# Group norm after retention: centring the value rows instead of the prompt's outputs

## Chip, core and metric

The kernel is one launch on one core of a Trainium2 chip. The metric is the device time of the launch in microseconds; lower is better. Three executions of the kernel before gave 679.87, 680.28 and 681.02 us, a median of 680.28 us.

## What is computed

A step of a two-layer hybrid network over 256 prompt tokens and 8 sample tokens, all in float32. Each layer has an input projection, three branches (a diagonal state-space model, called S5, stick-breaking attention, and retention), an output projection, a layer norm and a gated convolutional feed-forward with another layer norm. The change is in retention and the group norm behind it:

```python
def retention_chunk(s, q, k, v):
    ...
    inner = jnp.einsum('blhd,bmhd->bhlm', q, k) * decay
    o = jnp.einsum('bhlm,bmhe->blhe', inner, v)
    ...
def retention_branch(q, k, v, g, pos, s0, gn_g, gn_b):
    ...
    mu = jnp.mean(o, -1, keepdims=True)
    var = jnp.mean(jnp.square(o - mu), -1, keepdims=True)
    o = ((o - mu) * lax.rsqrt(var + LN_EPS)).reshape(bn, L, RET_WIDTH) * gn_g + gn_b
    return jax.nn.silu(g) * o, s_new
```

There are 4 heads with 128 values each (`e` above). For the prompt the starting state is zero, so an output row is a weighted sum of value rows. For the samples the old state, of 64 x 128 per head, is added.

## The kernel before, in words

Activations lie transposed: 128 features on the partitions, T = 264 tokens on the free axis (columns 0 to 255 the prompt, 256 to 263 the samples). A weight unit is a 128 x 1024 piece of weights. Units come by DMA into a ring of five buffers (`ring`). ScalarE casts a unit to `w_hi` (`split_hi`) and VectorE subtracts to get `w_lo` (`split_lo`), and each product is then three matmuls, on lines 429 to 431. The 20 units of the input projection are the exception: most go straight from the ring (line 422), four in layer 1 are split early (`EARLY`, lines 441 to 443).

Everything is written out by hand, engine by engine: each engine has its own program, in its own order, and semaphores tie them. `need(engine, name, L, k)` waits until `name` has been counted k times in layer L. `claim(bank, reader, ...)` makes TensorE wait until the last reader of a PSUM bank is done. The table `AT` says after which unit of the input projection each piece of the branches is put. No planner moves anything.

Names that the steps below use:

- `transposes` (TensorE, lines 568 to 575) turns the prompt's values into token rows in banks 4 and 5; `v_tokens` (ScalarE, line 1134) copies them to `VT`.
- `s5_glu` puts two products in banks 2 and 3, and ScalarE reads both with a sigmoid (line 1236). `k_transposes` (line 593) claims bank 2 afterwards, `v_samples` (line 584) follows it on TensorE.
- `ret_out` (lines 656, 657) multiplies the decayed scores `RI` with `VT`; ScalarE copies the outputs to `Oh` (line 1264). `ret_samples_turn` (line 648) turns the samples' part in bank 6, and `sample_out` (VectorE, lines 1762, 1766) adds it into `Oh` and frees the bank (`osamp`).
- `gn_means` (line 665) multiplies `Oh` with a matrix of 1/128 in four banks. `gn_center` (line 1863) subtracts the result, ScalarE squares (line 1278) and `gn_vars` (line 671) averages the squares.
- `square_sum` (line 1868) and `rms` (line 566) do the norms of the other two branches in the same stretch.
- `conv_prev` (lines 1804 to 1807) prepares the samples' old convolution rows, `spre`, which the feed-forward stage reads some 40 us later.
- The branches' results are split into `cat_hi` (ScalarE, line 1155) and `cat_lo` (VectorE, line 1881), eight pieces each. The output projection (lines 429 to 431) takes its first three units over pieces 0 to 3, then over 4 to 7, and waits for each piece of `cat_lo`.

Of the kernel before, what the change touches and what calls it, by code (L numbers as in the profile page):

```python
# [24 lines left out]
ALU = mybir.AluOpType  # L25
ACT = mybir.ActivationFunctionType

P = 128
SEQ, NS = 256, 8
T = SEQ + NS  # L30
# [76 lines left out]
def hybrid_step(nc, A, O):  # L107
    with ExitStack() as ctx:
# [53 lines left out]
        we_hi = [at(f"we_hi{e}", [P, 8, P], over=(home, plane * HJ * T), dt=F32R)  # L162
                 for e, (home, plane) in enumerate((("work", 0), ("work", 1), ("turn", 0), ("turn", 1)))]
        tabs = [(turn[:, 0, :, 0:SEQ], turn[:, 1, :, 0:SEQ]), None]
        RI = at("RI", [P, HEADS, DEC])
        KD = at("KD", [P, 2, 256])
# [46 lines left out]
        steps = at("steps", [P, SEQ])  # L213
        kdec = at("kdec", [P, 2, HEADS])
        gam = at("gam", [P, 1])
        gcol = at("gcol", [P, RAW, 2])
# [49 lines left out]
        def need(eng, name, L, k):  # L266

            eng.wait_ge(S(name), L * PERL[name] + k)

        def in_bank(i):  # L270
# [7 lines left out]
                "vb": 2, "vbev": 2, "rin": 4, "ri": 4, "rstate": 1, "rso": 1, "srg": 1, "sr": 1, "qs": 5,  # L278
                "rsq": 1, "otev": 1, "rot": 1, "osamp": 1, "ro": 4, "oev": 4, "gmean": 4, "gd": 4, "gsq": 4,
                "gvar": 4, "gv1": 1, "gr": 1, "gsil": 2,  # L280
# [119 lines left out]
        def _(pe):  # L400
# [250 lines left out]
            def ret_out(L):  # L651
                need(pe, "vt", L, 2)
                for h in range(HEADS):
                    need(pe, "ri", L, h + 1)
                    bank = claim(OUT_BANK[h], "oev", L, h + 1)
                    mm(bank[:, 0:SEQ], VT[:, 0, h * DV:(h + 1) * DV], RI[:, h, 0:SEQ], start=True, stop=False)
                    E.did(mm(bank[:, P:SEQ], VT[:, 1, h * DV:(h + 1) * DV], RI[:, h, SEQ:DEC], start=False, stop=True),
                          "ro")

            def gn_means(L):  # L660
                need(pe, "osamp", L, 1)
                for h in range(HEADS):
                    need(pe, "oev", L, h + 1)
                    bank = claim(4 + h, "gd", L, h + 1)
                    E.did(mm(bank[:, 0:T], C["mean_v"], Oh[:, h], start=True, stop=True), "gmean")  # L665

            def gn_vars(L):
                for h in range(HEADS):
                    need(pe, "gsq", L, h + 1)
                    bank = claim(4 + h, "gv1", L, 1)  # L670
                    E.did(mm(bank[:, 0:T], C["mean_v"], sqo[:, h], start=True, stop=True), "gvar")  # L671
# [94 lines left out]

            pe.wait_ge(S("warm"), 1)
            warm(WARM[0])
# [4 lines left out]
            for L in range(DEPTH):  # L773
# [7 lines left out]
                for i in range(RAW, N_IN):  # L781
# [41 lines left out]
                    if L == 0 and i == at_["out"]:  # L823
                        ret_out(L)
                    if i == at_["rt"]:
                        ret_samples_turn(L)
                    if i == at_["yt"]:
                        sb_values_turn(L)
                    if L > 0 and i == at_["vt"]:
                        transposes(L)  # L830
                    if L > 0 and i == at_["out"]:
# [93 lines left out]
        def _(act):  # L925
# [14 lines left out]
            def split_hi_early(L, i):  # L940

                n = L * UNITS + i
                act.wait_ge(S(f"ld_w{ring_slot(n)}"), 16 * (n // RING + 1))
                need(act, "s5rd", L, 2)
                E.did(nc.scalar.copy(we_hi[EARLY[L].index(i)][:], ring[:, ring_slot(n)]), "w_hi")

# [183 lines left out]
            def v_tokens(L):  # L1130

                for tt in range(2):
                    need(act, "trv", L, tt + 1)
                    E.did(nc.scalar.copy(VT[:, tt], ps[:, 4 + tt]), "vt")

# [36 lines left out]
            logs()  # L1172
            act.wait_ge(S("eps_set"), 5)
            s5_params(0, 0)
            s5_params(0, 1)
            for L in range(DEPTH):
                at_ = AT[L]
                ln_in(L)
                for i in range(RAW, N_IN):
# [172 lines left out]
        def _(dve):  # L1352
# [3 lines left out]

            E.did(nc.vector.memset(sq2[:, 0], 0.0), "warm")
            E.did(nc.vector.memset(eps_all[:, 0:1], LN_EPS), "eps_set")
# [500 lines left out]

            def gn_center(L, heads):  # L1860
                for h in heads:
                    need(dve, "gmean", L, h + 1)
                    E.did(tt(Oh[:, h], Oh[:, h], ps[:, 4 + h, 0:T], ALU.subtract), "gd")

# [13 lines left out]
            def branch_lo(L, k):  # L1878

                need(dve, "cat_hi", L, k + 1)  # L1880
                E.did(tt(cat_lo[:, k], cat[k], cat_hi[:, k].bitcast(F32), ALU.subtract), "cat_lo")

# [33 lines left out]
            for L in range(DEPTH):  # L1916
# [35 lines left out]
                if EARLY[L]:  # L1952
                    split_lo_early(L, EARLY[L][0])
                sb_out(L)
                if EARLY[L]:
                    lower_early(L, 1)
                conv_prev(L)
                for e in EARLY[L][1:]:
                    split_lo_early(L, e)
                if L == 0:  # L1960
                    split_lo(L, N_IN)
                    ret_states(L, range(0, STATES[L][0]))
                else:
                    split_lo(L, N_IN)
                    split_lo(L, N_IN + 1)
                sample_out(L)
                sb_sample_out(L)
                if L > 0:
                    split_lo(L, N_IN + 2)
                    ret_states(L, range(0, STATES[L][0]))  # L1970
                square_sum(L, 0)
                gn_center(L, (0, 1))
                square_sum(L, 1)
                gn_center(L, (2, 3))
                if L == 0:
                    split_lo(L, N_IN + 1)
                ret_states(L, range(STATES[L][0], STATES[L][1]))
                s5_cat(L)
                sb_cat(L)
# [226 lines left out]
```

## Time and profile before

| what | value |
|---|---|
| median of three runs | 680.28 us |
| the profiled execution, whole | 679.98 us |
| its span, from first to last instruction | 678.2 us |
| mean granted TensorE clock | 0.997 |
| stretch of layer 0 with retention and its norm | about 95 to 126 us |
| the same stretch in layer 1 | about 411 to 454 us |

Times in the trace are microseconds from the start of the span. In a timeline a row is one instruction or a run of like ones: its start, its length, the engine, the line and the tiles, and in brackets how long the engine sat idle before it and what ended that. A float32 matmul is recorded as two, so "x8" on TensorE (PE) is four matmuls. PEld is its weight load. Instructions on one engine overlap by about 0.1 us, so the next may start before the row's end.

### The profile page before, as it was taken

The numbers are of one execution on the slowest core, as the hardware profiler recorded it, in microseconds if no ns is written. First come the engines' busy times: TensorE is split into PE (matmuls) and PEld (weight loads), VectorE is DVE, ScalarE is ACT, GpSimd is POOL, SyncE is SP. The second block draws the span as 40 slices with busy tenths as digits, with TensorE's granted clock in tenths as the row PEclk, the third lists the DMA queues.
The fourth block names the chain that finished last, engine by engine and source line by source line (L and its number), as shares of the span: only waits on it lengthen the run. The fifth ranks groups of instructions, "written<-read, shape, count | busy, mean of one in ns | idle before, by whom it ended". The sixth has DMA issues, their size and how long they took to land.

```text
span 678.2 us, 13570 instructions
## 1 busy us (share of the span) xinstructions
PE 662.4 (98%) x5128; PEld 614.8 (91%) x5128; DVE 567.7 (84%) x1191; ACT 416.4 (61%) x681; POOL 85.9 (13%) x82
## 2 busy tenths in 40 slices
PE   8999999999999999999998999999999999999994
PEld 6777887989999999999976787999999999999994
DVE  6998998989998988789489998698999898884754
ACT  5776258757676666645746445687767666663343
POOL 0000000140221212200200000005012222220011
PEclk9999999999999999999999999999999999999998
DMA  9776520746674655554356473264766555556511
GB/s 322 225 279 222 197 79 5 280 109 222 212 246 155 214 185 173 187 187 156 125 180 225 171 219 105 70 242 133 193 211 201 184 174 194 176 185 195 160 50 65
DMA packets 42100, 120.59 MB, mean 178 GB/s; under 512 B 5362, under 2 KB 14482, under 8 KB 41522
## 3 DMA queue, kind: packets, MB, share of 16 engines
q1 hardware_dynamic: 40322, 115.02, 50.9%
q0 software_dynamic: 704, 3.06, 2.0%
q10 hardware_dynamic: 1008, 1.63, 0.7%
q8 instruction: 41, 0.67, 0.4%
q14 instruction: 25, 0.20, 0.1%
HBM read 114.21 MB, written 5.48 MB: 176 GB/s over the span
## 4 chain that ended last, share of the span: by engine, by line
PE 83%; DVE 11%; ACT 2%; DMA 1%; issue 1%; SPq 0%; DVEq 0%
PE ps L429 21%; PE ps L430 21%; PE ps L431 21%; PE ps L422 10%; DVE z L1429 2%; DVE z L1437 2%; DMA z<-in_xT 1%; PE ps L481 1%; PE ps L544 1%; PE ps L584 1%; PE ps L665 1%; PE ps L750 1%; PE ps L671 1%; PE ps L559 1%; PE ps L716 1%
## 5 line engine op out<-in xcount | busy, mean ns | idle before, releaser
L1523 DVE TENSOR_TENSOR w_lo<-ring,w_hi 128x1024 fp32r<-128x1024 f32 x144 | 175.6, 1221 | 39.2 <-ACT w_hi L938 37.6
L429 PE MATMUL ps<-x_hi,w_hi 128*128 128x264 f32 x672 | 191.0, 284 | 1.0 <-DVE x_lo L1475 1.0
L430 PE MATMUL ps<-x_lo,w_hi 128*128 128x264 f32 x672 | 190.4, 283 | 0.0
L431 PE MATMUL ps<-x_hi,w_lo 128*128 128x264 f32 x672 | 190.3, 283 | 0.0
L938 ACT CAST w_hi<-ring 128x1024 fp32r<-128x1024 f32 x144 | 150.1, 1042 | 64.3 <-PE ps L431 61.8
L429 PEld LDWEIGHTS ps<-x_hi,w_hi 128*128 128x128 f32 x672 | 126.5, 188 | 1.8 <-issue 1.8
L430 PEld LDWEIGHTS ps<-x_lo,w_hi 128*128 128x128 f32 x672 | 126.6, 188 | 0.0
L431 PEld LDWEIGHTS ps<-x_hi,w_lo 128*128 128x128 f32 x672 | 126.0, 187 | 0.0
L422 PE MATMUL ps<-x,ring 128*128 128x264 f32 x480 | 112.2, 390 | 0.0
L422 PEld LDWEIGHTS ps<-x,ring 128*128 128x128 f32 x480 | 89.1, 190 | 19.1 <-issue 2.2
L429 PE MATMUL ps<-hff_hi,w_hi 128*128 128x264 f32 x352 | 100.4, 285 | 0.0
L431 PE MATMUL ps<-hff_hi,w_lo 128*128 128x264 f32 x352 | 99.9, 284 | 0.0
L430 PE MATMUL ps<-hff_lo,w_hi 128*128 128x264 f32 x352 | 99.9, 284 | 0.0
L2085 POOL TENSOR_TENSOR hff_lo<-conv,hff_hi 128x264 fp32r<-128x264 f32 x44 | 52.7, 1199 | 214.7 <-ACT hff_hi L1168 214.7
L431 PEld LDWEIGHTS ps<-hff_hi,w_lo 128*128 128x128 f32 x352 | 66.3, 188 | 0.0
L429 PEld LDWEIGHTS ps<-hff_hi,w_hi 128*128 128x128 f32 x352 | 66.2, 188 | 0.1
L430 PEld LDWEIGHTS ps<-hff_lo,w_hi 128*128 128x128 f32 x352 | 66.2, 188 | 0.1
L1318 ACT ACTIVATE conv<-ps,vec 128x264 f32<-128x264 f32 x84 | 47.8, 569 | 22.5 <-PE ps L431 22.5
L1168 ACT CAST hff_hi<-conv 128x264 fp32r<-128x264 f32 x44 | 18.2, 414 | 47.5 <-DVE conv L1544 47.4
L2025 DVE SCALAR_TENSOR_TENSOR conv<-ps,vec,conv 128x254 f32<-128x254 f32 x84 | 40.5, 482 | 3.0
L1183 ACT COPY hb<-ps 128x264 f32<-128x264 f32 x34 | 12.7, 374 | 46.2 <-PE ps L422 44.9
L2022 DVE SCALAR_TENSOR_TENSOR conv<-ps,vec,conv 128x255 f32<-128x255 f32 x84 | 39.8, 474 | 0.0
(338 smaller groups left out, 1083.4 us busy)
## 6 DMA issues: line engine op xcount, KB each, us to landing
ring<-in_units SPq DMA_DIRECT2D x187, 512.0 KB, 3.7
kv<-in_kpool SPq DMA_DIRECT2D x32, 128.0 KB, 2.2
kv<-in_vpool SPq DMA_DIRECT2D x32, 128.0 KB, 2.4
SR<-in_sret SPq DMA_DIRECT2D x2, 1024.0 KB, 6.4
out_rsample<-SR POOLq DMA_DIRECT2D x2, 1024.0 KB, 4.9
out_kv<-hb ACTq DMA_DIRECT2D x2, 528.0 KB, 4.5
out_y<-x SPq DMA_DIRECT2D x3, 264.0 KB, 2.0
prev<-in_prev SPq DMA_DIRECT2D x2, 352.0 KB, 4.5
```

The source lines that it names most:

```text
L422: ins = mm(out, ring[:, ring_slot(n), k], rhs(k), start=(k == 0), stop=(k == 7))
L429: mm(out, wh, hi, start=start, stop=False)
L430: mm(out, wh, lo, start=False, stop=False)
L431: return mm(out, wl, hi, start=False, stop=stop)
L938: E.did(nc.scalar.copy(w_hi[:, split_slot(i)], ring[:, ring_slot(n)]), "w_hi")
L1168: E.did(nc.scalar.copy(hff_hi[:, p], conv[:, (2 * p + 1) % CSLOTS]), "hff_hi")
L1318: E.did(f(conv[:, i % CSLOTS], source, ACT.Identity, scale=pv(L, "cw2", i), bias=pv(L, "cb", i)), "fc")
L1429: E.did(tt(z[:, t0:t1], z[:, t0:t1], mean, ALU.subtract))
L1523: E.did(tt(w_lo[:, slot], ring[:, ring_slot(L * UNITS + i)], w_hi[:, slot].bitcast(F32), ALU.subtract), "w_lo")
L2022: E.did(stt(c[:, 1:SEQ], bank[:, 0:SEQ - 1], pv(L, "cw1", i), c[:, 1:SEQ], ALU.mult, ALU.add))
L2025: E.did(stt(c[:, 2:SEQ], bank[:, 0:SEQ - 2], pv(L, "cw0", i), c[:, 2:SEQ], ALU.mult, ALU.add), "up_free")
L2085: E.did(tt(hff_lo[:, p], conv[:, (2 * p + 1) % CSLOTS], hff_hi[:, p].bitcast(F32), ALU.subtract), "hff_lo")
```

## The change

The mean over e of an output row is the same weighted sum of the means of the value rows. The new kernel subtracts each value row's mean from that row, once, before the output matmuls. The prompt's outputs then have mean zero and need no centring. Samples still have the old state in them, so they keep the mean and the subtraction, on 32 columns instead of 1056.

- ScalarE's copy to `VT` is made in eight pieces of 128 columns (4 heads, 2 token blocks), each also writing the sum of its rows, `vsum`.
- VectorE makes `VTc` from `VT` and `vsum` in two instructions of 128 x 512 (`center_values`), and `ret_out` uses `VTc`. The state matmuls (`ret_state`) still use `VT`.
- `gn_means` is one matmul of 32 columns, `gn_center` one instruction of 32 columns. The four squares of 264 columns become two of 2 x 256 (prompt) and one of 32 (samples), under one count, and every variance matmul waits for that count.
- In layer 0 `conv_prev` moves from before `split_lo(N_IN)` to just before `s5_cat`.
- In layer 1 the value transposes are issued ahead of two other transposes, and `split_lo(L, N_IN + 1)` moves behind `sample_out`.
- `VTc` takes the place of one of the early weight buffers, which moves to a plane that `rotary` uses; so the early casts also wait for `qk`.

```diff
+        VTc = at("VTc", [P, 2, HEADS * DV], over=("turn", HJ * T))
...
             def ret_out(L):
-                need(pe, "vt", L, 2)
+                need(pe, "vtc", L, 2)
...
-                    mm(bank[:, 0:SEQ], VT[:, 0, h * DV:(h + 1) * DV], RI[:, h, 0:SEQ], start=True, stop=False)
+                    mm(bank[:, 0:SEQ], VTc[:, 0, h * DV:(h + 1) * DV], RI[:, h, 0:SEQ], start=True, stop=False)
...
             def gn_means(L):
                 need(pe, "osamp", L, 1)
-                for h in range(HEADS):
-                    need(pe, "oev", L, h + 1)
-                    bank = claim(4 + h, "gd", L, h + 1)
-                    E.did(mm(bank[:, 0:T], C["mean_v"], Oh[:, h], start=True, stop=True), "gmean")
+                bank = claim(4, "gd", L, 1)
+                E.did(mm(bank[:, 0:HEADS * NS], C["mean_v"], Oh[:, :, SEQ:T], start=True, stop=True), "gmean")
 
             def gn_vars(L):
                 for h in range(HEADS):
-                    need(pe, "gsq", L, h + 1)
+                    need(pe, "gsq", L, 1)
...
+                    if L > 0 and i == at_["vt"]:
+                        transposes(L)
                     if i == at_["rt"]:
                         ret_samples_turn(L)
                     if i == at_["yt"]:
                         sb_values_turn(L)
-                    if L > 0 and i == at_["vt"]:
-                        transposes(L)
...
                 need(act, "s5rd", L, 2)
+                need(act, "qk", L, 1)
...
-                    E.did(nc.scalar.copy(VT[:, tt], ps[:, 4 + tt]), "vt")
+                    for h in range(HEADS):
+                        part = slice(h * DV, (h + 1) * DV)
+                        ins = f(VT[:, tt, part], ps[:, 4 + tt, part], ACT.Copy, accum_out=vsum[:, tt, h:h + 1])
+                    E.did(ins, "vt")
...
-                        for h in range(HEADS):
-                            need(act, "gd", L, h + 1)
-                            E.did(f(sqo[:, h], Oh[:, h], ACT.Square), "gsq")
+                        act.wait_ge(S("oev"), HEADS * (L + 1))
+                        for h in (0, 2):
+                            E.did(f(sqo[:, h:h + 2, 0:SEQ], Oh[:, h:h + 2, 0:SEQ], ACT.Square))
+                        need(act, "gd", L, 1)
+                        E.did(f(sqo[:, :, SEQ:T], Oh[:, :, SEQ:T], ACT.Square), "gsq")
...
+            def center_values(L):
+
+                for k in range(2):
+                    need(dve, "vt", L, k + 1)
+                    E.did(stt(VTc[:, k].rearrange("p (h e) -> p h e", h=HEADS), bcast(vsum[:, k], [P, HEADS, DV], 2),
+                              -1.0 / DV, VT[:, k].rearrange("p (h e) -> p h e", h=HEADS), ALU.mult, ALU.add), "vtc")
```

VectorE, layer 0, from the first `square_sum` to the first instruction of `s5_cat`. Before:

```order
L1868 TENSOR_TENSOR sqa<-sqa 128x264
L1863 TENSOR_TENSOR Oh<-Oh,ps 128x264 x2
L1868 TENSOR_TENSOR sq_108<-sq_108 128x264
L1863 TENSOR_TENSOR Oh<-Oh,ps 128x264 x2
L1523 TENSOR_TENSOR w_lo<-ring,w_hi 128x1024
L1793 SCALAR_TENSOR_TENSOR SR<-VBC,hb,SR 128x128 x4
L1894 SCALAR_TENSOR_TENSOR hb<-yg,vec,rms_113 128x264 x2
```

The same place in the changed kernel, whose line numbers are 6 to 15 higher here:

```order
L1881 TENSOR_TENSOR sqa<-sqa 128x264
L1876 TENSOR_TENSOR Oh<-Oh,ps 128x4x8
L1881 TENSOR_TENSOR sq_109<-sq_109 128x264
L1529 TENSOR_TENSOR w_lo<-ring,w_hi 128x1024
L1799 SCALAR_TENSOR_TENSOR SR<-VBC,hb,SR 128x128 x4
L1810 TENSOR_TENSOR spre<-prev,vec 128x352
L1811 TENSOR_TENSOR cout<-prev,vec 128x44x8
L1813 TENSOR_TENSOR spre<-spre,cout 128x352
L1909 SCALAR_TENSOR_TENSOR hb<-yg,vec,rms_114 128x264 x2
```

Four centrings have become one small one, and the three instructions of `conv_prev` have come in behind `ret_states`.

ScalarE, layer 0, between the S5 gelu and the sigmoid that frees banks 2 and 3. Before:

```order
L1233 ACTIVATE yg<-yd 128x528
L1134 COPY VT<-ps 128x512 x2
L1183 COPY hb<-ps 128x264
L1236 ACT_TABLE_LOAD
L1236 ACTIVATE sq_108<-ps 128x528
```

After:

```order
L1237 ACTIVATE yg<-yd 128x528
L1137 ACTIVATE VT,vsum<-ps 128x128 x8
L1187 COPY hb<-ps 128x264
L1240 ACT_TABLE_LOAD
L1240 ACTIVATE sq_109<-ps 128x528
```

Two copies have become eight with a second output; nothing else in this piece moved.

VectorE, layer 1, from `split_lo(L, N_IN)` to the first `ret_states`. Before:

```order
L1523 TENSOR_TENSOR w_lo<-ring,w_hi 128x1024 x2
L1762 TENSOR_TENSOR Oh<-hb,ps 128x4x8
L1766 TENSOR_TENSOR Oh<-Oh,ps 128x4x8
L1852 COPY yb<-ps 64x8 x4
L1523 TENSOR_TENSOR w_lo<-ring,w_hi 128x1024
L1793 SCALAR_TENSOR_TENSOR SR<-VBC,hb,SR 128x128 x8
```

After:

```order
L1529 TENSOR_TENSOR w_lo<-ring,w_hi 128x1024
L1870 SCALAR_TENSOR_TENSOR VTc<-vsum,VT 128x512 x2
L1768 TENSOR_TENSOR Oh<-hb,ps 128x4x8
L1772 TENSOR_TENSOR Oh<-Oh,ps 128x4x8
L1858 COPY yb<-ps 64x8 x4
L1529 TENSOR_TENSOR w_lo<-ring,w_hi 128x1024 x2
L1799 SCALAR_TENSOR_TENSOR SR<-VBC,hb,SR 128x128 x8
```

The centring of the values stands where the second `w_lo` stood, and that `w_lo` now comes after the samples' outputs.

## Rows read from the trace of the kernel before

**Rows 1.** The page: busy time, share of the span and instructions, by engine.

```profile
PE 662.4 (98%) x5128; PEld 614.8 (91%) x5128; DVE 567.7 (84%) x1191; ACT 416.4 (61%) x681; POOL 85.9 (13%) x82
```

**Rows 2.** Timeline of TensorE, the means and variances of both layers.

```profile
110.58 2.05 PE L665 MATMUL ps<-Oh,cst 128*128 128x264 f32 x8
...
113.44 1.94 PE L671 MATMUL ps<-RI,cst 128*128 128x264 f32 x8
...
442.04 1.94 PE L671 MATMUL ps<-RI,cst 128*128 128x264 f32 x8
```

**Rows 3.** Timeline of ScalarE, layer 0, value copies to attention outputs.

```profile
95.61 1.05 ACT L1134 COPY VT<-ps 128x512 f32<-128x512 f32 x2
...
98.26 0.61 ACT L1236 ACTIVATE sq<-ps 128x528 f32<-128x528 f32 x1
...
105.40 0.58 ACT L1247 COPY ysb<-ps 128x512 f32<-128x512 f32 x1 [1.97 <-PE ps L750]
```

**Rows 4.** Groups of ScalarE by form: busy us, mean ns of one.

```profile
L1264 ACT COPY Oh<-ps 128x256 f32<-128x256 f32 x8 | 2.9, 374 | 2.4 <-PE ps L657 2.4
...
L1134 ACT COPY VT<-ps 128x512 f32<-128x512 f32 x4 | 2.1, 584 | 0.7 <-PE ps L573 0.7
...
L984 ACT COPY zg<-vec 128x16 f32<-128x16 f32 x4 | 0.8, 210 | 0.2
```

**Rows 5.** Timeline of TensorE's weight loads, layer 0: behind the sigmoid, output projection.

```profile
99.27 0.42 PEld L593 LDWEIGHTS ps<-cst,hb 128*128 128x128 f32 x4
100.04 1.69 PEld L584 LDWEIGHTS ps<-cst,hb 128*32 128x32 f32 x64 [0.34 <-DVE RI L1783]
...
119.94 0.19 PEld L429 LDWEIGHTS ps<-cat_hi,w_hi 128*128 128x128 f32 x1 [0.17 <-issue]
```

**Rows 6.** Timeline of ScalarE, layer 0, the square ahead of the group norm's.

```profile
111.48 0.64 ACT L1275 ACTIVATE sq<-yb 128x528 f32<-128x528 f32 x1
```

**Rows 7.** Timeline of VectorE, layer 0, from `conv_prev` to `cat_lo`.

```profile
104.01 0.51 DVE L1804 TENSOR_TENSOR spre<-prev,vec 128x352 f32<-128x352 f32 x1
...
106.96 1.22 DVE L1523 TENSOR_TENSOR w_lo<-ring,w_hi 128x1024 fp32r<-128x1024 f32 x1 [1.44 <-ACT w_hi L938]
...
111.72 0.77 DVE L1863 TENSOR_TENSOR Oh<-Oh,ps 128x264 f32<-128x264 f32 x2
112.41 0.42 DVE L1868 TENSOR_TENSOR sq<-sq 128x264 f32<-128x264 f32 x1
...
115.62 0.89 DVE L1894 SCALAR_TENSOR_TENSOR hb<-yg,vec,rms 128x264 f32<-128x264 f32 x2
...
119.87 0.76 DVE L1881 TENSOR_TENSOR cat_lo<-hb,cat_hi 128x264 fp32r<-128x264 f32 x2
```

**Rows 8.** Timelines and ring loads of layer 1, around `ret_out` and the squares.

```profile
427.60 1.07 ACT L1134 COPY VT<-ps 128x512 f32<-128x512 f32 x2 [0.71 <-PE ps L573]
...
429.92 1.05 ACT L938 CAST w_hi<-ring 128x1024 fp32r<-128x1024 f32 x1 [1.25 <-DMA ring<-in_units]
...
430.76 0.59 PE L656 MATMUL ps<-RI,VT 128*128 128x256 f32 x2
...
431.01 1.23 DVE L1523 TENSOR_TENSOR w_lo<-ring,w_hi 128x1024 fp32r<-128x1024 f32 x1 [3.44 <-ACT w_hi L938]
...
430.95 0.33 SPq L346 DMA_DIRECT2D ring<-in_units  x1
...
DMA to landing us min/median/max: 3.3/3.3/3.4
...
432.70 0.67 PE L656 MATMUL ps<-RI,VT 128*128 128x256 f32 x2 [0.47 <-DVE Oh L1766]
...
435.50 1.29 ACT L1139 COPY VBC<-ps 128x512 f32<-128x512 f32 x2
...
440.33 0.65 ACT L1275 ACTIVATE sq<-yb 128x528 f32<-128x528 f32 x1
```

**Rows 9.** One window: us, PE busy, PEld, DVE, ACT, POOL, granted clock, DMA.

```profile
360.00:364.00 4.00, 2.79 (x37) 1.60 (x36) 3.97 (x4) 0.40 (x2) 0.00 (x0) 1.00 0.80 273
```

More of the change, by code:

```diff
@@ L162, in hybrid_step @@
         we_hi = [at(f"we_hi{e}", [P, 8, P], over=(home, plane * HJ * T), dt=F32R)
-                 for e, (home, plane) in enumerate((("work", 0), ("work", 1), ("turn", 0), ("turn", 1)))]
+                 for e, (home, plane) in enumerate((("work", 0), ("work", 1), ("turn", 0), ("work", 3)))]
         tabs = [(turn[:, 0, :, 0:SEQ], turn[:, 1, :, 0:SEQ]), None]
+        VTc = at("VTc", [P, 2, HEADS * DV], over=("turn", HJ * T))
         RI = at("RI", [P, HEADS, DEC])
@@ L214, in hybrid_step @@
         kdec = at("kdec", [P, 2, HEADS])
+        vsum = at("vsum", [P, 2, HEADS])
         gam = at("gam", [P, 1])
@@ L278, in hybrid_step @@
                 "vb": 2, "vbev": 2, "rin": 4, "ri": 4, "rstate": 1, "rso": 1, "srg": 1, "sr": 1, "qs": 5,
-                "rsq": 1, "otev": 1, "rot": 1, "osamp": 1, "ro": 4, "oev": 4, "gmean": 4, "gd": 4, "gsq": 4,
+                "rsq": 1, "otev": 1, "rot": 1, "osamp": 1, "ro": 4, "oev": 4, "gmean": 1, "gd": 1, "gsq": 1, "vtc": 2,
                 "gvar": 4, "gv1": 1, "gr": 1, "gsil": 2,
@@ L655, in ret_out @@
                     bank = claim(OUT_BANK[h], "oev", L, h + 1)
-                    mm(bank[:, 0:SEQ], VT[:, 0, h * DV:(h + 1) * DV], RI[:, h, 0:SEQ], start=True, stop=False)
-                    E.did(mm(bank[:, P:SEQ], VT[:, 1, h * DV:(h + 1) * DV], RI[:, h, SEQ:DEC], start=False, stop=True),
+                    mm(bank[:, 0:SEQ], VTc[:, 0, h * DV:(h + 1) * DV], RI[:, h, 0:SEQ], start=True, stop=False)
+                    E.did(mm(bank[:, P:SEQ], VTc[:, 1, h * DV:(h + 1) * DV], RI[:, h, SEQ:DEC], start=False, stop=True),
                           "ro")
@@ L765, in warm @@
                     mm(ps[:, 7, 0:T], sq2[:, 0, 0:P], sq2[:, 0], start=True, stop=True)
-            pe.wait_ge(S("warm"), 1)
+            pe.wait_ge(S("eps_set"), 1)
             warm(WARM[0])
@@ L1172, in _ @@
             logs()
-            act.wait_ge(S("eps_set"), 5)
+            act.wait_ge(S("eps_set"), 6)
             s5_params(0, 0)
@@ L1355, in _ @@
             cp = nc.vector.tensor_copy
-            E.did(nc.vector.memset(sq2[:, 0], 0.0), "warm")
+            E.did(nc.vector.memset(sq2[:, 0], 0.0), "eps_set")
             E.did(nc.vector.memset(eps_all[:, 0:1], LN_EPS), "eps_set")
@@ L1858, in sb_cat, with gn_center @@
                     E.did(stt(hb[:, QB_ + t], yb[:, t], pv(L, "norm_b_g", t), rms2[:, 1], ALU.mult, ALU.mult), "catb")
[L1860 to L1863, printed above, removed]
+            def center_values(L):
[3 more added lines that the diff above has]
+                              -1.0 / DV, VT[:, k].rearrange("p (h e) -> p h e", h=HEADS), ALU.mult, ALU.add), "vtc")
+            def gn_center(L):
+                need(dve, "gmean", L, 1)
+                o = Oh[:, :, SEQ:T]
+                E.did(tt(o, o, ps[:, 4, 0:HEADS * NS].rearrange("p (h b) -> p h b", h=HEADS), ALU.subtract), "gd")
             def square_sum(L, part):
@@ L1880, in branch_lo @@
                 need(dve, "cat_hi", L, k + 1)
+                if k == 4 and EARLY[L]:
+                    tile_done(dve, L, EARLY[L][-1])
                 E.did(tt(cat_lo[:, k], cat[k], cat_hi[:, k].bitcast(F32), ALU.subtract), "cat_lo")
@@ L1953, in _ @@
                     split_lo_early(L, EARLY[L][0])
+                if L == 0:
+                    center_values(L)
                 sb_out(L)
@@ L1956, in _ @@
                     lower_early(L, 1)
-                conv_prev(L)
+                if L > 0:
+                    conv_prev(L)
                 for e in EARLY[L][1:]:
@@ L1964, in _ @@
                     split_lo(L, N_IN)
-                    split_lo(L, N_IN + 1)
+                    center_values(L)
                 sample_out(L)
@@ L1968, in _ @@
                 if L > 0:
+                    split_lo(L, N_IN + 1)
                     split_lo(L, N_IN + 2)
@@ L1971, in _ @@
                 square_sum(L, 0)
-                gn_center(L, (0, 1))
+                gn_center(L)
                 square_sum(L, 1)
-                gn_center(L, (2, 3))
                 if L == 0:
@@ L1977, in _ @@
                 ret_states(L, range(STATES[L][0], STATES[L][1]))
+                if L == 0:
+                    conv_prev(L)
                 s5_cat(L)
```

## Prediction, made blind

> **What bounds the kernel now.** The page comes first: TensorE is busy in 98% of the span, VectorE in 84, ScalarE in 61 [rows 1]. A microsecond taken from TensorE counts only where nothing else ends last a moment later, so the stage is read from the timelines. The four mean matmuls take about 2 us in each layer [rows 2]. The question is what has to be ready when they are gone. The variance matmuls start at 113.44 and 442.04 [rows 2], and they need ScalarE's squares. ScalarE squares `yb` from 111.48 in layer 0 and from 440.33 in layer 1 [rows 6, 8], and only then the heads. VectorE works almost without a break up to `cat_lo`, which the output projection waits for [rows 7].
>
> **Layer 0, the value copies.** The two copies of 512 columns take 1.05 together [rows 3] and 0.584 each alone [rows 4], so two neighbours overlap by 0.11. The step from one instruction to the next is then 0.47 at 512 columns and 0.26 at 256 (0.374 - 0.11) [rows 4]. On that line a copy of 128 has a step of 0.16. What the row sum adds no row shows. It may be nothing. At most I take one more smallest ScalarE instruction for each piece: 0.21 long [rows 4], a step of 0.10 with the overlap. I take the step, so 0.26 a piece, 8 x 0.26 + 0.11 = 2.2 us, 1.15 more than before. The bounds are 0.16 a piece (1.4 us, 0.35 more) and 0.16 + 0.21 = 0.37 (3.1 us, 2.0 more).
>
> The Trainium skill, page "VectorE: DVE Perf Modes", section "Two Vector instructions with no wait between them", says that a Vector operation that also writes out its accumulator is two instructions; if ScalarE does likewise, the price is above zero. The page "ScalarE: Activation LUTs", section "What ACT_TABLE_LOAD costs", gives 186 ns plus 0.833 ns a column, with 93 ns of overlap. By it 256 columns take 399 ns, and the row has 374. A step at 128 columns would be 0.20, and the sum below would be 0.3 us higher.
>
> Behind the copies stand the evacuation of unit 18, a table load and the sigmoid, which ended at 98.87 [rows 3] and now ends at 100.0. `k_transposes` claims the bank that the sigmoid reads and loaded its weights at 99.27 [rows 5]; it had 0.35 to spare and now starts 0.8 late. `v_samples` waited for VectorE before it started at 100.04 [rows 5]; that wait of about 0.2 goes. **TensorE loses 0.6 us** (bounds 0 and 1.5). ScalarE itself has caught up by 105.40, where it stood idle for 1.97 waiting for TensorE [rows 3].
>
> `center_values` is two instructions of 512 columns. Rows have 0.77 for two neighbours of 264 columns and 1.22 for one of 1024 [rows 7], so about 0.7 each, 1.3 together. They replace `conv_prev`, which ran from 104.01 until VectorE went idle at 105.52 (1.5 us), and 1.44 of idle time stand behind it [rows 7]. So they cost nothing; without that cover `ret_out` would be 1.3 later.
>
> **Layer 0, the norm.** The matmul of 32 columns is worth 0.1 to 0.3 instead of 2.05. ScalarE decides the rest. From 111.48 [rows 6] four squares follow: 528, 512, 512 and 32 columns. The first takes 0.64, and with the overlap steps are 0.55: 111.48 + 3 x 0.55 + 0.2 = 113.33. All four variance matmuls wait for that one count. With 0.05 for the signal they start at 113.38, against 113.44 [rows 2]. **Of the 1.8 us taken from TensorE, 0.06 comes back**; the rest is a wait.
>
> VectorE: `square_sum` on `yb` started at 112.41 and can start when ScalarE's square ends, 112.17, 0.24 earlier; the second pair of centrings goes (0.69, the step of the first pair, 111.72 to 112.41) [rows 7]. That is 0.93 saved. `conv_prev` comes in with 1.45. So `s5_cat` moves from 115.62 to 116.1, and as VectorE runs on without idle time up to `cat_lo`, the piece `cat_lo` 2, ready at 119.87 + 0.43 = 120.3 [rows 7], is ready at 120.8. TensorE starts the output projection at 119.94 [rows 5], now 119.9, and takes 0.36 a piece (nine weight loads at 0.12 each make three), so it wants piece 2 at 120.6. **It waits 0.25.** The later pieces had 0.45 or more to spare and hold. If `conv_prev` had stayed, this term would be nought. Net for the norm of layer 0: +0.2.
>
> **Layer 1.** The transposes go first, 0.66 earlier. The eight copies start at 426.9 (they began at 427.60 after a wait of 0.71) [rows 8] and end at 429.1. The cast behind them waited for its weights until 429.92 anyway [rows 8], so they cost nothing there. `center_values` ends at 429.8, before `ret_out` at 430.76 (at the upper bound 430.7, just in time). VectorE had stood idle for 3.44 until 431.01 in front of the second `w_lo`, and the samples' outputs behind it held up `ret_out`'s third head by 0.47, 0.6 with the weight load [rows 8]. That wait goes. But the next cast on ScalarE needs the unit that is issued at 430.95 and takes 3.3 to 3.4 [rows 8], so it can start at 434.35 where it started at 434.55. The copies behind it began at 435.50 and took 1.29 where two neighbours take 1.07; they now start at 435.3 and end at 436.37 instead of 436.79. So the square of `yb` moves from 440.33 [rows 8] to 439.91, and the variance matmuls start at 439.91 + 1.65 + 0.2 + 0.05 = 441.81 instead of 442.04. **Gain 0.23.** VectorE has time in this layer, for `conv_prev` did not move there.
>
> **The rest.** The wait for `qk` in front of the early casts costs nothing: the rotary instructions are done well before them. The same holds for the wait for unit 19 in front of `cat_lo` 4, and `spre` in layer 0 is read 40 us later. No transfer is added, no queue's order changes.
>
> **Sum:** 0.6 + 0.2 - 0.23 = +0.6 us. The profiled execution took 679.98, 0.3 below the median, so it would be 680.6; on the median 680.28 the changed kernel is at **680.9 us**.
>
> **Rivals.**
> 1. *The row sum is dear.* If a piece costs 0.37, TensorE loses 1.5 in layer 0, and the sum is 1.5 + 0.2 - 0.2 = +1.5: 681.8. If nothing overlaps (0.265 + 0.21 = 0.48), the copies take 3.9, TensorE loses 2.4, and `center_values` in layer 1 ends at 431.5, which eats the gain there and more: +2.8, 683.1. It decides "slower" from 0.36 a piece. For it: a short read-out behind a longer instruction may have to wait until that has drained. Against it: neighbours overlap in all rows I read. Chance 0.24.
> 2. *TensorE does get its matmuls back.* If the squares of the prompt were not in the way, TensorE would gain 1.8 in layer 0 and 1.6 in layer 1, and 0.6 with the wait in `ret_out`; less 0.6 for the copies and 0.2 at `cat_lo`: -3.2, 677.1. For it: the work really leaves a 98% engine. Against it: [rows 6, 8], ScalarE's squares end where the means ended. Half of it, with shorter squares of 2 x 256, gives 678.7. Chance 0.20 for both.
> 3. *The clock.* TensorE now has holes of up to 0.9 us between the norms' matmuls. If its clock fell to 1.2 GHz for the next 4 us, that would be 2 us more a layer. In 360 to 364 it is busy for only 2.79 of 4.00 and stays at 1.00 [rows 9], so I give it 0.02 (684).
>
> **How the numbers follow.** The likeliest case, 0.54, has a range of its own from the bounds of the copies: 680.0 to 681.8. I take 678.4 to 682.8, which leaves out the full gain, half of rival 1's dear end and the clock, some 2 in 10. No change that can be told is within 0.2%, 1.36 us. "Faster" is rival 2, 0.20. "Slower" is rivals 1 and 3 above +1.36, 0.25. "Same" is 0.55.
>
> **What the profile of the changed kernel would show.** Right: the eight copies take about 2.2 us; `k_transposes` starts 0.8 late behind the sigmoid; variance matmuls start right behind ScalarE's last square, with TensorE idle ahead of them, in both layers; the output projection of layer 0 waits for `cat_lo`; `ret_out` in layer 1 has no wait. Wrong: squares that end well before 113.3 on this scale, copies above 2.9 us, or a wait for `VTc`.

## The result, and the profile after

The changed kernel took 682.62 us in the median of 16 executions (681.06 to 684.19), the kernel before 680.17 in as many (679.26 to 681.54). The ratio is 1.0033, with a 95% interval of 1.0027 to 1.0040: slower, by 2.4 us between the medians, and by more than the 0.2% that can be told apart from noise. The forecast was 680.9, within a range of 678.4 to 682.8; the result lies at its upper edge, and outside the 680.0 to 681.8 of the likeliest case.

The profiled execution took 681.3 us, 1.3 below that median, with a span of 679.4 and a mean granted clock of 0.995. It shows about half of the loss. The page's busy times, to be held against [rows 1]:

```profile
PE 661.5 (97%) x5116; PEld 613.5 (90%) x5116; DVE 568.8 (84%) x1189; ACT 418.4 (62%) x707; POOL 86.6 (13%) x82
```

TensorE has lost work, and the span is 1.2 longer, so it waits more. Where, the timelines tell. First ScalarE in layer 0, where [rows 3] were (a row: start, length, engine, line, what, and in brackets the idle time before it and what ended that):

```profile
95.66 0.26 ACT L1137 ACTIVATE VT<-ps 128x128 f32<-128x128 f32 x1
95.82 0.20 ACT L1137 ACTIVATION_READ_ACCUMULATOR VT<-ps 128x1 f32 x1
95.91 0.27 ACT L1137 ACTIVATE VT<-ps 128x128 f32<-128x128 f32 x1
...
97.57 0.25 ACT L1137 ACTIVATION_READ_ACCUMULATOR VT<-ps 128x1 f32 x1
...
99.40 0.61 ACT L1240 ACTIVATE sq<-ps 128x528 f32<-128x528 f32 x1
...
112.16 0.64 ACT L1279 ACTIVATE sq<-yb 128x528 f32<-128x528 f32 x1
112.71 1.13 ACT L1282 ACTIVATE RI<-Oh 128x512 f32<-128x512 f32 x2
113.75 0.21 ACT L1284 ACTIVATE RI<-Oh 128x32 f32<-128x32 f32 x1
```

A piece is two instructions, the copy and a read-out of the sum, the step from piece to piece is 0.25, and the last ends at 97.82. The sigmoid ends at 100.01. TensorE's weight loads in the same layer, where [rows 2, 5] were:

```profile
100.13 0.42 PEld L595 LDWEIGHTS ps<-cst,hb 128*128 128x128 f32 x4 [0.70 <-issue]
100.72 1.69 PEld L586 LDWEIGHTS ps<-cst,hb 128*32 128x32 f32 x64 [0.17 <-issue]
...
111.25 0.30 PEld L665 LDWEIGHTS ps<-Oh,cst 128*128 128x128 f32 x2 [0.37 <-DVE Oh L1772]
112.42 0.30 PEld L568 LDWEIGHTS ps<-sqa,cst 128*128 128x128 f32 x2 [0.88 <-DVE sqa L1881]
113.32 0.30 PEld L568 LDWEIGHTS ps<-sq,cst 128*128 128x128 f32 x2 [0.60 <-DVE sq L1881]
114.01 1.63 PEld L671 LDWEIGHTS ps<-RI,cst 128*128 128x128 f32 x8 [0.39 <-ACT RI L1284]
...
129.86 0.30 PEld L451 LDWEIGHTS ps<-z,cst 128*128 128x128 f32 x2 [0.25 <-DVE z L1914]
148.19 0.30 PEld L518 LDWEIGHTS ps<-acc,cst 128*128 128x128 f32 x2 [0.85 <-DVE acc L1410]
...
403.65 0.59 PEld L546 LDWEIGHTS ps<-work,cf 128*32 128x32 f32 x16 [0.57 <-DVE sfin L1740]
...
443.09 1.63 PEld L671 LDWEIGHTS ps<-RI,cst 128*128 128x128 f32 x8 [0.39 <-ACT RI L1284]
```

Between the small mean matmul and the variances TensorE now stands idle for 0.88, 0.60 and 0.39 us; such an idle time between its matmuls is called a hole below. Two waits for VectorE follow that no term of the forecast had, at the layer norm behind the stage (L451, L518). The second was there before, but shorter, as the row of the kernel before shows, together with a load wait in layer 1 that comes up below:

```profile
146.55 0.30 PEld L516 LDWEIGHTS ps<-acc,cst 128*128 128x128 f32 x2 [0.37 <-DVE acc L1404]
...
361.96 1.48 PEld L698 LDWEIGHTS ps<-kv,qz 128*32 128x32 f32 x32 [1.60 <-issue]
```

So TensorE's lateness against the kernel before is, by the starts of its weight loads: 0.86 at `k_transposes`, 0.68 at `v_samples`, and 1.64 at L518 (148.19 less 146.55). In layer 1 it is 1.13 at the S5 read-out (L546; 402.52 in the kernel before, with no wait), 1.27 at the variances, where the kernel before loads at 441.82, and 1.2 at the end. At the start of layer 0's output projection it is still 0.68 (120.62 against 119.94): the norm itself cost and gave nothing.

Layer 1, ScalarE, where [rows 8] were:

```profile
435.68 1.05 ACT L938 CAST w_hi<-ring 128x1024 fp32r<-128x1024 f32 x1 [0.61 <-DMA ring<-in_units]
436.63 1.07 ACT L1143 COPY VBC<-ps 128x512 f32<-128x512 f32 x2
...
441.24 0.65 ACT L1279 ACTIVATE sq<-yb 128x528 f32<-128x528 f32 x1
```

### The profile page after: what moved, and what is told of

Read it like the earlier page. It is cut to its first block and busy times, and to the rows that moved or that the text cites. A ratio compares the mean times of both kernels' runs of the same rounds, so it can differ in the third digit from the quotient of the medians.

```text
span 679.4 us, 13565 instructions
## 1 busy us (share of the span) xinstructions
PE 661.5 (97%) x5116; PEld 613.5 (90%) x5116; DVE 568.8 (84%) x1189; ACT 418.4 (62%) x707; POOL 86.6 (13%) x82
## 3 DMA queue, kind: packets, MB, share of 16 engines
q10 hardware_dynamic: 1008, 1.63, 0.7%
```

## The experiments

All ten kernels ran beside executions of the kernel before (medians 680.01 in the first four, 680.08 in the next four, 680.06 in the last two). Each execution has its mean granted clock, the share of full speed that TensorE was granted over the whole span, and that number turned out to sort them: no execution of the kernel before, 83 in these three sets, is below 0.995. The table is put together from the results; "clock fell" counts executions with 0.993 or 0.994.

```
kernel                                  median   95% of ratio       clock fell
before                                  680.0-680.2                 0 of 83 (27, 35, 21)
changed                                 682.62   1.0027 to 1.0040   9 of 16
after_again  changed, again             683.00   1.0028 to 1.0055   4 of 5
fill         fillers in the holes       681.41   1.0008 to 1.0026   0 of 11
conv_back    conv_prev back             680.97   1.0007 to 1.0028   3 of 11
conv_fill    both                       681.02   1.0004 to 1.0022   0 of 11
pieces       before, eight copies       680.41   0.9997 to 1.0015   0 of 11
narrow       before, cut means          680.40   1.0000 to 1.0017   5 of 12
delay0       before, 2 more matmuls     680.57   0.9998 to 1.0015   0 of 11
early        squares out of the way     678.61   0.9967 to 0.9985   0 of 11
early2       the same, put right        678.09   0.9963 to 0.9981   0 of 11
early2_conv  that, conv_prev late       679.77   0.9986 to 1.0004   0 of 11
```

**The changed kernel again** (no edit).

> The changed kernel, unchanged, run again as the yardstick of the others; the question is its spread. Clock theory (about half of the executions lose 2 us because TensorE's holes in the norm stage let its granted clock fall): executions fall into a group near 681.3 with a mean clock of 0.995 and one near 683.4 with 0.993 or 0.994, while the kernel before stays in one group within 0.7 us of 680.2. Path theory (the whole loss is longer waits): one group near 682.6, with no step in the clock between its faster and slower executions.

Measured: 683.00; executions at 682.23, 683.00, 683.09 and 683.26 with a clock of 0.993, one at 682.30 with 0.995. The last does not fit the expected group near 681.3, and here the two kinds lie only 0.7 apart; with five executions that says little. The kernel before spread by up to 1.1 from 680.0 beside it, more than expected, but with no clock below 0.995. The profile of the changed kernel caught the fall. Two stretches of layer 0, TensorE (stretch, its length, PE busy, granted clock, DMA share, GB/s), and the weight loads of the variances:

```profile
110.00:114.00 4.00, 2.92 (x16) 1.00 0.02 4
114.00:118.00 4.00, 4.00 (x11) 0.57 0.00 0
...
114.24 2.92 PEld L671 LDWEIGHTS ps<-RI,cst 128*128 128x128 f32 x8 [0.40 <-ACT RI L1284]
```

The first profile has the same waits ahead of it, 0.88, 0.60 and 0.39, and at 1.00 it takes 1.63 for these loads:

```profile
114.00:118.00 4.00, 4.00 (x19) 1.00 0.00 0
```

So the same 1.1 us of idle TensorE between 110 and 114 is followed by 1.2 GHz in one execution and by 2.4 GHz in the other. A clock of 0.57 over these 4 us is 1.7 us of clock lost. The loads of `ret_state` started at 121.46 against 119.55, and as the variances had started 0.23 later already, they have lost 1.7 us there.

Most of that does not last. The load at the layer norm, which waited 0.85 in the first profile, does not wait in this one:

```profile
148.81 0.41 PEld L518 LDWEIGHTS ps<-acc,cst 128*128 128x128 f32 x2
```

Against the first profile TensorE is 1.9 late at `ret_state`, but 0.62 here (148.81 against 148.19), because VectorE, which the first profile waited for, brings its `acc` only 0.24 later (147.94 against 147.70). Up to the stage of the `kv` wait 0.72 is left (357.66 against 356.94), of which 0.23 was there before the fall. So a fall at this place costs about 0.5 us in the end, and the rest of the 0.9 by which this execution is longer than the first is not the fall's: it was 0.23 late before, and the `kv` wait in layer 1, described below, was 0.76 longer (1.28 against 0.52), part of which was made up behind it.

**Fillers in the holes.**

```diff
+            def filler(L, n):
+                need(pe, "oev", L, HEADS)
+                for _ in range(n):
+                    mm(ps[:, 5, 0:SEQ], C["mean_v"], Oh[:, 0, 0:SEQ], start=True, stop=True)
...
+                        filler(L, 2)
                         rms(L, sqa, 1, "rmsl", "rms", 2)
+                        filler(L, 2)
                         rms(L, sq2, 2, "rmsl", "rms", 3)
```

> The changed kernel with four more matmuls of 256 columns in each layer's norm stage, two ahead of each root mean square; their result is never read, and everything else is untouched. They put TensorE to work in the holes of 0.88, 0.60 and 0.39 us. Clock theory: the slower group of executions goes, and the median falls by 1 to 1.5 us, to 681.2 to 681.6, at a mean clock of 0.995 or above. Path theory: nothing to gain; same time or up to 0.3 us a layer slower, 682.6 to 683.2, since the fillers can only delay the root mean squares.

Measured: 681.41, 1.2 to 1.6 below the changed kernel; no execution above 681.78, none with a fallen clock. Eight matmuls of work that nobody reads make the kernel faster, as the clock theory had it. They cost little on the path: the variances' loads start at 114.46 instead of 114.01, but this execution was 0.39 late at `v_samples` already (101.11 against 100.72), so 0.06 is the fillers'; in layer 1 it is 0.23, from 0.07 late at the mean matmul to 0.30 at the variances.

**Less work, more holes** (the kernel before, with the means cut to the samples' columns; the prompt's means are left out and VectorE subtracts what the banks held, so it stands here for its time alone).

```diff
-                    E.did(mm(bank[:, 0:T], C["mean_v"], Oh[:, h], start=True, stop=True), "gmean")
+                    E.did(mm(bank[:, SEQ:T], C["mean_v"], Oh[:, h, SEQ:T], start=True, stop=True), "gmean")
```

> The kernel before, with its four mean matmuls cut to the samples' 8 columns each; the prompt's columns are not averaged, and VectorE subtracts what the banks held. Every other instruction stays. TensorE has 1.5 us less to do in each layer and stands idle instead. Path theory: the variance matmuls end up to 0.6 us earlier in each layer, 679.2 to 680.1 in all, no slower executions. Clock theory: less work, but holes of 0.4 and 0.8 us, so that some executions lose 1.5 to 2 us behind them and show a mean clock of 0.993 or 0.994; a median up to 681.5.

Measured: 680.40. Five of its twelve executions have a clock of 0.993 and take 680.76 to 682.05, the other seven 0.995 or above and 679.28 to 680.57. The kernel before showed this in none of 35 beside it. The profile, of an execution whose clock did not fall, has holes of 0.20 and 0.84 in layer 0 and of 1.35 in layer 1, where the kernel before has 0.23 and 0.46. So holes bring the fall without any other part of the change; their groups' medians, 681.38 and 679.91, differ by 1.5. For the changed kernel, in the 16 executions, it is 683.39 and 681.3: 2.1.

**The convolution rows back in place.**

```diff
-                if L > 0:
-                    conv_prev(L)
+                conv_prev(L)
...
-                if L == 0:
-                    conv_prev(L)
                 s5_cat(L)
```

> The changed kernel with the preparation of the samples' convolution rows put back where it stood in layer 0, ahead of the first low half. My reading: the output projection of layer 0 no longer waits for its third low piece (0.1 us in the profiled execution, 0.25 forecast), and nothing else changes, so 0.1 to 0.3 us faster than the changed kernel, 682.4 on its median. Rival reading: the place was chosen well, and back in its old one it delays the output matmuls by up to 1.3 us.

Measured: 680.97, 1.7 to 2.0 below the changed kernel, not 0.1 to 0.3. Part may be chance, since the clock fell in 3 of 11 here, with the same holes. Among executions whose clock did not fall, the median is 680.4 here and 681.3 in the changed kernel: 0.9 is the move's. Between the two profiles TensorE's loads are 1.24 apart at the layer norm (L518), and 0.08 of that was there before. It is in a row that the expectation left aside, the wait for `acc` in the layer norm, 0.16 where the changed kernel has 0.85:

```profile
146.95 0.30 PEld L518 LDWEIGHTS ps<-acc,cst 128*128 128x128 f32 x2 [0.16 <-DVE acc L1410]
```

In the changed kernel VectorE is behind, and TensorE runs into that 9 and 28 us behind the start of the output projection (120.62).

**Both edits together.** Edits as above.

> Both single edits together: the convolution rows back, and the filler matmuls ahead of the two root mean squares. If VectorE's lateness (0.9 us by the drift of its rows behind layer 0) and the fall of the clock (1.7 us in some executions) are two separate causes, the group of slower executions goes and the median lies at 680.5, no execution above 681.5. If the convolution rows alone had cured the clock, the fillers only cost: 681.0 to 681.3.

Measured: 681.02, between the two expectations: no fallen clock, but one execution at 682.37, and 0.5 more than the sum of two causes gave. Set against `conv_back` it gains nothing in the median. By the rows the fillers cost 0.05 in layer 0 and 0.2 in layer 1; why the rest is missing stays open. This one tells little.

**The copies alone** (the kernel before; the sums are written and not read).

```diff
-                    E.did(nc.scalar.copy(VT[:, tt], ps[:, 4 + tt]), "vt")
+                    for h in range(HEADS):
+                        part = slice(h * DV, (h + 1) * DV)
+                        ins = f(VT[:, tt, part], ps[:, 4 + tt, part], ACT.Copy, accum_out=vsum[:, tt, h:h + 1])
+                    E.did(ins, "vt")
```

> The kernel before with one edit: the two value copies are made in eight pieces with row sums, and nothing reads the sums. It has the cost of the copies alone. My step for layer 0 says that TensorE loses 0.6 us behind the sigmoid; layer 1 has slack. So 680.8, and no step in the clock, since the norm stage has no new holes. If most of the changed kernel's loss is in the copies (rival 1), it is at 682 or above. If the copies are hidden, 680.2.

Measured: 680.41, 0.4 above the kernel before, not told from no change. Rival 1, the dear row sum, is out, by the rows too: the step from piece to piece is 0.25, not 0.37. Its `v_samples` starts at 100.97 in an execution that was 0.28 late at 92 us already, so 0.65 of it is the copies', as forecast.

**Layer 0 one microsecond later.**

```diff
+                    if L == 0 and h == 0:
+                        for _ in range(2):
+                            mm(bank[:, 0:T], C["mean_v"], Oh[:, h], start=True, stop=True)
```

> The kernel before with the first mean matmul of layer 0 issued three times over, the same result each time: everything behind it in layer 0 is 1.0 us later, on TensorE, ScalarE and VectorE alike, with no new hole. Theory that layer 1 takes up part of what layer 0 loses (TensorE stands 1.60 us at the sample scores of layer 1 in the profile before, and starts the states' read-out 0.55 after VectorE is ready): the end moves by 0.4 to 0.5 us, to 680.5. Rival, that lateness is carried to the end in full: 681.1.

Measured: 680.57, 0.5 more, the number expected, but the interval takes in both no change and, at its edge, the rival's 681.1. The reason is weaker, too: the variances' loads were 0.76 late, not 1.0, since the extra matmuls filled a wait of before in part. In layer 1 the row of `kv` follows:

```profile
362.23 1.48 PEld L701 LDWEIGHTS ps<-kv,qz 128*32 128x32 f32 x32 [1.25 <-issue]
```

Its wait is 0.35 shorter than before. But this wait, in front of the matmuls that need the sample keys `kv`, is 0.48 to 1.60 in the twelve profiles, and not in step with how late TensorE came (1.60 in the kernel before, 0.52 in the changed one, 1.43 with fillers, 0.48 in `early2`). The rows of SyncE, which issues the loads of `kv` and of the weight units one behind the other, tell what it follows. The kernel before, and then `early2`:

```profile
344.63 1.52 SPq L346 DMA_DIRECT2D ring<-in_units  x1
...
356.62 3.62 SPq L354 DMA_DIRECT2D kv<-in_kpool  x4
...
344.45 0.43 SPq L348 DMA_DIRECT2D ring<-in_units  x1
...
355.35 3.61 SPq L356 DMA_DIRECT2D kv<-in_kpool  x4
```

The weight loads start 1.69 to 1.84 behind the end of the last `kv` issue in eleven of the twelve profiles (2.15 in `conv_back`): 1.72 in the first of these, 1.71 in the second. And the issue of one weight unit ahead of them took 0.43 in five profiles, whose waits are 0.48 to 0.93, and 1.10 to 1.52 in seven, whose waits are 1.25 to 1.60. Both occur with one and the same program: 0.43 in the first profile of the changed kernel, 1.10 in the second. What makes it long, no run shows. In `delay0` it was 1.20, 0.32 shorter than in the kernel before, so the shorter wait there need not be lateness taken up. How much layer 1 takes up on average is not settled.

**The squares out of the way.** The squares depend on data that is ready long before, so they move into ScalarE's idle times, and the sums into VectorE's:

```diff
                     if i == at_["sv"]:
+                        if L == 0:
+                            square_a(L)
+                            need(act, "ybev", L, 2)
+                            square_yb(L, slice(0, SEQ))
                         need(act, "sbys", L, 1)
...
+                            if L == 0 and h == 1:
+                                square_heads(L, 0)
                         if L == 0:
-                            square_a(L)
+                            square_heads(L, 2, "gsq")
+                            need(act, "ybs", L, 1)
+                            square_yb(L, slice(SEQ, T))
+                            need(act, "gd", L, 1)
+                            E.did(f(sqo[:, :, SEQ:T], Oh[:, :, SEQ:T], ACT.Square), "gsq")
+                        else:
+                            square_heads(L, 0)
                         split_hi(L, N_IN + 2)
```

> The changed kernel with the samples' convolution rows back in their old place, and with ScalarE's squares taken out of the way of the variance matmuls. Layer 0: the squares of yg and of yb's prompt columns go into ScalarE's idle 1.50 us ahead of the ysb copy, the first pair of heads behind the second output copy, the samples' columns of yb and Oh are squared by two small instructions, and the cast that stood ahead of them goes behind; VectorE adds the squares in its idle 0.67 us. Layer 1: yb's prompt columns are squared while ScalarE waits for a weight unit, the first pair of heads ahead of the next cast, VectorE adds in its idle 3.3 us. From the rows of the run with only the convolution rows put back, the variance matmuls can start at 112.3 instead of 113.94 in layer 0, where VectorE's own row gives 0.9 us, and at 440.2 instead of 441.72 in layer 1. Theory that ScalarE's order ate the gain: 2 us better than that run's 680.97, about 679.0, and faster than the kernel before. Rival, that VectorE or the weight transfers are the bound of these stretches: 680.5 or more. Clock: the holes shrink to 0.4 us in layer 0, so no execution should show a fall there.

Measured: 678.61, 0.24% faster than the kernel before. In layer 0 the variances started at 113.28 only, as the early square held up what stood behind it; in layer 1 at 440.41. The next kernel puts that right:

```diff
-                            need(act, "ybev", L, 2)
-                            square_yb(L, slice(0, SEQ))
                         need(act, "sbys", L, 1)
...
                             if L == 0 and h == 1:
-                                square_heads(L, 0)
+                                need(act, "ybev", L, 2)
+                                square_yb(L, slice(0, SEQ))
                         if L == 0:
+                            square_heads(L, 0)
                             square_heads(L, 2, "gsq")
```

> The last kernel with one correction in layer 0: the square of yb's prompt columns had stood ahead of the ysb copy and made it, the two casts and the output copies behind it 0.33 us later. It moves behind the second output copy, both pairs of heads follow the fourth, and VectorE adds behind its third pair of state updates, where it waits anyway. If that 0.33 us and the wait of 0.63 us at the second root mean square are all that was lost, layer 0 gains 0.4 us and the median is 678.2; if layer 1 takes it up (TensorE waits 1.40 us at the sample scores there), it is 678.6, no change.

Measured: 678.09, 0.28% faster than the kernel before and 4.5 us faster than the changed one, with the same arithmetic. Its weight loads:

```profile
111.52 0.30 PEld L665 LDWEIGHTS ps<-Oh,cst 128*128 128x128 f32 x2 [0.37 <-DVE Oh L1791]
...
112.67 0.30 PEld L568 LDWEIGHTS ps<-sq,cst 128*128 128x128 f32 x2 [0.63 <-DVE sq L1900]
...
439.56 1.63 PEld L671 LDWEIGHTS ps<-RI,cst 128*128 128x128 f32 x8 [1.08 <-ACT RI L1302]
```

In layer 0 one wait of 0.63 is left of the three, in layer 1 one of 1.08, and the variances of layer 1 load 3.5 us earlier than in the changed kernel. Both executions had a short `kv` wait (0.48 and 0.52), so this is the path's: 1.9 us by the load at L518 (146.30 against 148.19), and the rest in layer 1. Between the medians of executions without a fallen clock it is 3.2 (678.1 against 681.3); the other 1.3 of the 4.5 come with the falls. The convolution rows are part of it: against `conv_back`, where they too stand in their old place, the squares' new places alone bring 2.3 (680.4 without a fall).

**The price of the moved rows alone** (`early2`, with `conv_prev` of layer 0 ahead of `s5_cat`).

```diff
-                conv_prev(L)
+                if L > 0:
+                    conv_prev(L)
...
+                if L == 0:
+                    conv_prev(L)
                 s5_cat(L)
```

> The same kernel with the samples' convolution rows of layer 0 in the place that the change gave them, ahead of s5_cat; the price of that move alone, with the other costs out of the way. My forecast took it for a wait of 0.25 us at the output projection and nothing behind it: 0.25 more. By the drift of VectorE's rows it is VectorE's whole 1.2 us, which TensorE meets at the layer norm of layer 0 (the waits for z and for acc), less what layer 1 takes up: 0.6 to 1.2 more.

Measured: 679.77, 1.7 us more (0.25 was forecast, 0.6 to 1.2 expected). No clock fell in either kernel, so the clock has no part in it. Three waits of its profile, none of which `early2` has at this length:

```profile
120.39 0.19 PEld L431 LDWEIGHTS ps<-cat_hi,w_hi 128*128 128x128 f32 x1 [0.25 <-DVE cat_lo L1915]
128.71 0.30 PEld L451 LDWEIGHTS ps<-z,cst 128*128 128x128 f32 x2 [0.25 <-DVE z L1933]
...
147.23 0.30 PEld L518 LDWEIGHTS ps<-acc,cst 128*128 128x128 f32 x2 [1.03 <-DVE acc L1429]
```

The first is the forecast's wait, to the digit. The other two stand behind it, and `early2` waits 0.33 at the last. TensorE's loads there start 0.93 later, though this execution had been 0.5 ahead at the variances: 1.4 lost by there. The `kv` wait then was 1.47 against 0.48, and that one varies by itself; the two profiled executions end 1.4 apart. So of the 1.7 between the medians the rows show 1.4 as the move's, and the changed kernel against `conv_back` gave 0.9 between executions without a fall and 1.2 by the rows.

## Why the prediction was right or wrong

**The copies: right.** 2.2 us for eight, from 95.66 to 97.82 (forecast 2.2), a step of 0.25 (0.26), `k_transposes` 0.86 late (0.8), `v_samples` 0.68 (0.6). That the sum is read out by an instruction of its own is seen in the rows: 0.16 of the step is the copy's and 0.09 the read-out's, which is 0.20 to 0.25 long (forecast 0.16 and 0.10).

**The variances of layer 0: right.** The squares end at 113.96; the matmuls, now 0.68 late in all, start at 114.01. The 0.06 that was to come back is 0.1 by that start and nothing by the unit behind them, which starts 0.68 late (115.90 against 115.22). The work taken from TensorE did turn into waits.

**`conv_prev`: wrong step.** "If `conv_prev` had stayed, this term would be nought. Net for the norm of layer 0: +0.2." The wait for `cat_lo` exists (0.25 in `early2_conv`; in the changed kernel the first load of the third piece starts 0.32 behind the load ahead of it, where the usual step is 0.12), and the step stopped there. From 112.83 to 131 VectorE has a single idle 0.52 us, ahead of a weight split at 126.66 whose cast stands in ScalarE's queue behind VectorE's own outputs, so a piece of 1.45 us put into that stretch stays in its queue, and TensorE meets it again at `z` (0.25) and at `acc` (0.85 for 0.37). In its old place the 1.45 stood in front of idle time and cost nothing, as the prediction itself said. In place of the 0.25 it costs 0.9 us by the executions without a fallen clock, and 1.7 by the pair `early2` and `early2_conv`.

**Layer 1: mis-sized.** The gain of 0.23 hung on a weight unit landing 3.3 to 3.4 after its issue. ScalarE waited for it until 435.68; TensorE was 1.13 late in layer 1 at the S5 read-out, and without that the cast is at 434.55, where it was, and not at 434.35. By the unit behind the variances, and less what TensorE brought along, the gain was 0 in this profile and 0.1 with `conv_back`. `ret_out` has no wait in either, as forecast. Besides, lateness from layer 0 was assumed to be carried over in full, and the `kv` wait, which follows SyncE's issues and not TensorE, adds or takes up a varying part.

**Rival 3, the clock: true in most executions, and given 0.02.** The step that failed: "In 360 to 364 it is busy for only 2.79 of 4.00 and stays at 1.00 [rows 9]". That row is true, and so is its like in the changed kernel, 2.92 of 4.00 and still 1.00 in the profiled execution. One profile shows one outcome of something that comes out differently from execution to execution: 13 of 21 fell. What was forecast for a fall, about 2 us, is what the groups differ by (2.1), but not by the mechanism forecast: the fall that a profile shows, in layer 0, takes 1.7 on the spot and leaves 0.5, since TensorE meets VectorE's lateness at the layer norm either way. Where the slower executions lose the rest is open. The Trainium skill, page "TensorE: Matmul & The Clock Gate", section "A second HAM failure mode: psum-queue depth-cycling", says that short idle times repeated between groups of matmuls made the clock of one kernel swing; the trace agrees that short ones are enough, with waits of 0.88, 0.60 and 0.39 and a clock of 0.57 over the next 4 us, though it shows one fall and no repeated swing. Whether the other executions' fall lies at the same place, or in layer 1, where the waits reach 1.63, no profile shows.

**Rival 2, that TensorE gets its matmuls back:** false for this change, and reachable. The forecast named its condition, squares that are not in the way; with that met, and `conv_prev` back in its old place, `early2` runs 2.0 us faster than the kernel before, where the rival had 3.2.

**The sum.** The forecast was +0.6: copies 0.6, `conv_prev` 0.25, layer 1 -0.23. Without a fallen clock the changed kernel is at 681.3, which is 1.1 above the kernel before. The copies alone gave 0.4, the move of `conv_prev` gave 0.9 among such executions, layer 1 nothing: 1.3, within the noise of the 1.1. The executions with a fallen clock, 9 of 16, are 2.1 longer in the median, which brings the whole to 682.62. "Same" was given 0.55 and "slower" 0.25; it is slower. That 682.62 still lies within the range is luck. Its upper end, 682.8, was set for dear copies, which were as cheap as forecast, and it left the clock out by intent; the clock and `conv_prev` took the time there.

## What to carry to other kernels

Work taken from the busiest engine comes back only if what it waits for next is moved too: here the change lost 2.4 us with the squares where they stood, and won 2.0 with the squares in ScalarE's idle times and the convolution rows in their old place. An instruction moved into a stretch in which its engine has no idle time must be followed past the first wait, to the next place where the queues meet, even 30 us on. And where holes open on TensorE, look at the clock of every execution and not at one profile; a few matmuls that nobody reads, or better an order without the holes, are the test.

## What the runs showed of the hardware

- TensorE at 2.4 GHz fell to 1.2 GHz behind 4 us in which it was busy for 2.92, its longest wait 0.88 (the second profile of the changed kernel); in another execution of the same program, with the same waits, it did not. Eight filler matmuls ended it (0 of 11), and cutting matmuls out of the kernel before brought it (5 of 12).
- That fall took 1.7 us on the spot and left 0.5 behind the next stretch in which TensorE waits for VectorE.
- A ScalarE copy with a row sum is recorded as two instructions, 0.26 to 0.32 us for 128 columns out of PSUM and 0.19 to 0.25 for the read-out, and eight of them follow each other at 0.25.
- The issue of one weight load on SyncE, at the same place of the program, took 0.43 us in five profiles and 1.10 to 1.52 in seven. The `kv` loads are issued behind it, and TensorE's wait in front of the matmuls that need them was 0.48 to 0.93 in the five and 1.25 to 1.60 in the seven.
